# Masks as matmuls, 32-row score products and half units in the two attention stages of a hybrid layer kernel

## The chip, the cores and the metric

One core of a Trainium2 chip. The metric is the device time of one execution in microseconds, less is better. Engines are TensorE (PE in the profile, its weight loads PEld), VectorE (DVE), ScalarE (ACT), GpSimd (POOL) and the DMA queues, mostly issued by SyncE (SP). Each engine works through its own instructions strictly in program order and waits on semaphores.

## What is computed

The kernel computes a two-layer block (512 tokens, 1024 channels) and a second block with gated linear attention and experts. The change lies in the mixers of the first block, which both layers run. A projection is split into four groups: an rwkv7 recurrence (A), differential attention (B), spatial gating (C) and forgetting attention (D), each with 4 heads of 64 channels.

```python
def block(i):            # differential attention, 128 queries
    mask = key_chunk[None, :] <= q_chunk[:, None]        # chunks of 64
    s1 = jnp.einsum('bhqd,bhkd->bhqk', q1b, k1) * scale  # d = 32
    s2 = jnp.einsum('bhqd,bhkd->bhqk', q2b, k2) * scale
    p1 = jax.nn.softmax(jnp.where(mask, s1, NEG_INF), axis=-1)
    p2 = jax.nn.softmax(jnp.where(mask, s2, NEG_INF), axis=-1)
    return jnp.einsum('bhqk,bhkd->bhqd', p1 - lam * p2, v)

def block(i):            # forgetting attention
    s = jnp.einsum('bhqd,bhkd->bhqk', qb, k) * scale + (Fq[..., :, None] - F[..., None, :])
    pr = jax.nn.softmax(jnp.where(key_pos[None, :] <= q_pos[:, None], s, NEG_INF), axis=-1)
    return jnp.einsum('bhqk,bhkd->bhqd', pr, v)

def step(state, inp):    # rwkv7, one token; the kernel takes chunks of 64
    sa = jnp.einsum('bhvk,bhk->bhv', state, -kk_t)
    state = state * w_t + sa[..., None] * b_t + v_t[..., None] * k_t
    return state, jnp.einsum('bhvk,bhk->bhv', state, r_t)
```

## The kernel before

`mixers` (L1812) runs four instruction streams on every engine: attention (0), rwkv (1), the modulation rows (2) and the opening of the output projection (3). Each stream is a Python generator per engine, and `run` (L588) steps them by a list of numbers, the plan. TensorE, ScalarE and VectorE follow the same plan, so a plan entry 0 means "the next piece of attention" on all three. GpSimd has a short plan of its own.

An attention stage has 16 units: 4 heads times 4 blocks of 128 queries. Unit u looks at 1, 2, 3 or 4 blocks of 128 keys, so its tiles are 128, 256, 384 or 512 columns wide. Between two units the plan puts one or two rwkv steps (`alternate`, L1464).

**Forgetting stage.** A unit is, in time: score matmul into one of two banks (`score`, L771), on VectorE the causal mask added to the diagonal block (L995) and the row maximum (L997), on ScalarE the exponential (L899), on VectorE reciprocal (L1006) and scaling (L1009), on TensorE transposes (L807), on ScalarE the copy of them (L910), on TensorE the sum of values (L790). Plan entry u makes TensorE do scores of u+2, sums of u-1, transposes of u; VectorE mask and maximum of u+1, then scaling of u; ScalarE the exponential of u+1, then the copy of u. The rwkv steps of this stage are the `MICRO` ones (L1144 and L1150 on TensorE, two heads' worth of 64x64 matmuls, with a VectorE and a ScalarE operation behind some of them; for instance L1422 and L1430).

**Differential stage.** The same with two maps per unit, m = 0 and 1: scores L820, mask L1027, maximum L1029, exponential L925, reciprocal and mixing L1037, L1039, L1042 and L1044 ("the normalisation"), transposes L846, copy L939, sums L831. There is one bank for each map, so a score of a unit waits for the exponential of the unit before on the same map:

```python
for m, lane in enumerate(lanes(h)):
    if u >= 1:
        eng.wait_ge(df["exped"], 2 * (u - 1) + m + 1)
    eng.matmul(PS(m)[:, 0:width(u)], d_q[lane][:, i * P:(i + 1) * P], c.p[:, T_B + 2 + h // 2, 0:width(u)], ...)
```

The product is over 32 channels, but `d_q[lane]` is a 128-row tile with zeros outside its 32 rows, which GpSimd clears and fills (`spread_lanes`, L679; waits at L708 and L712). Plan entry u makes TensorE do scores of u+1, sums of u-1, transposes of u; VectorE the normalisation of u, then masks and maxima of u+1; ScalarE the copy of u, then the exponentials of u+1.

The rwkv steps of this stage are three parts for each of 8 chunks. Part A: TensorE L1245 and L1247 (and from the second chunk on an output, L1230 to L1232), then ScalarE L1329. Part B: TensorE L1255 (and an output), then VectorE L1440. Part C: TensorE L1264 and L1266, then VectorE L1444, on which the next A waits. 24 parts are spread over 17 plan entries.

Of the kernel before, what the change touches and what calls it, by code (L numbers as in the profile page):

```python
# [62 lines left out]
         ("mask_causal", 128), ("mask_chunk", 128), ("scan", 512), ("m_ld", 512), ("m_ldT", 512), ("m_loT", 512),  # L63
# [547 lines left out]
def attention_stream(c, mod, nc):  # L611
# [8 lines left out]
    fx = {n: sem(f"fx_{n}") for n in ("scored", "masked", "maxed", "exped", "inv", "scaled", "turned", "copied", "summed",  # L620
                                      "out", "zeroed", "spread")}
    df = {n: sem(f"df_{n}") for n in ("lam_dve", "lam_exp", "lam", "scored", "masked", "maxed", "exped", "inv", "mixed",
# [24 lines left out]
    d_q = [VT(V_D), VT(V_C), at["w"](7), VT(V_C + 1)]  # L647
    lanes = lambda h: [2 * h % 4, 2 * h % 4 + 1]
    d_prob, d_prob_t = [[SC(0), SC(1)], [SC(2), c.p[:, T_D, :]]], [SC(3 + i) for i in range(2)]
# [14 lines left out]
    def pool():  # L664
# [14 lines left out]
        def spread_lanes(h):  # L679
            for lane in lanes(h):  # L680
                r = slice(32 * lane, 32 * lane + 32)
                chain(eng.tensor_copy(d_q[lane][r, :], c.p[r, T_B + h // 2, :]))

# [19 lines left out]
        eng.wait_ge(pr["roped"], 3 * NJ)  # L703
        eng.wait_ge(fx["summed"], NU // 2)
        eng.memset(d_q[0], 0.0).then_inc(fx["zeroed"], 1)
        eng.wait_ge(fx["scored"], 12)
        for lane in (1, 2):
            eng.memset(d_q[lane], 0.0).then_inc(fx["zeroed"], 1)  # L708
        eng.wait_ge(fx["zeroed"], 8)
        spread_lanes(0)  # L710
        eng.wait_ge(fx["scored"], 16)
        eng.memset(d_q[3], 0.0).then_inc(fx["zeroed"], 1)  # L712
        eng.wait_ge(fx["zeroed"], 9)
        spread_lanes(1)
        yield
        for h in range(2, 4):
            eng.wait_ge(df["scored"], 8 * (h - 1))
            spread_lanes(h)
        yield

    def pe():
# [73 lines left out]
        for u in range(NU):  # L795
# [39 lines left out]
        for u in range(NU):  # L835
            if u == 0:
                score2(0)
            if u + 1 < NU:
                score2(u + 1)
# [5 lines left out]
            for b in range(blocks[u][1] + 1):  # L845
                last = eng.transpose(PS(2)[:, b * P:(b + 1) * P], d_prob[u % 2][0][:, b * P:(b + 1) * P], c.const("ident"))  # L846
            last.then_inc(df["turned"], 1)
            yield
        sum_values2(NU - 1)
# [7 lines left out]
    def act():  # L857
# [44 lines left out]
        for u in range(NU):  # L902
            if u == 0:
                exp(0)
            if u + 1 < NU:
                exp(u + 1)
            eng.wait_ge(fx["turned"], u + 1)
# [6 lines left out]
            yield  # L914
        eng.wait_ge(fx["summed"], NU)
# [3 lines left out]
        def exp2(u):  # L919
            for m in range(2):  # L920
                n = 2 * u + m
                eng.wait_ge(df["maxed"], n + 1)
                if u >= 2:
                    eng.wait_ge(df["turned"], u - 1)
                on(d_prob[u % 2][m][:, 0:width(u)], PS(m)[:, 0:width(u)], ACT.Exp, bias=d_max[:, n:n + 1],  # L925
# [7 lines left out]
        for u in range(NU):  # L933
            if u == 0:
                exp2(0)
            eng.wait_ge(df["turned"], u + 1)
# [5 lines left out]
            if u + 1 < NU:  # L942
                exp2(u + 1)
            yield
        take(1)
# [9 lines left out]
    def dve():  # L955
# [35 lines left out]
        def maximum(u):  # L991
            i = blocks[u][1]
            eng.wait_ge(fx["scored"], u + 1)
            diagonal = PS(u % 2)[:, i * P:(i + 1) * P]
            eng.tensor_tensor(diagonal, diagonal, c.const("mask_causal"), ALU.add).then_inc(fx["masked"], 1)  # L995
            eng.wait_ge(fx["masked"], u + 1)
# [3 lines left out]
        for u in range(NU):  # L1000
            if u == 0:
                maximum(0)
            if u + 1 < NU:
                maximum(u + 1)
            eng.wait_ge(fx["exped"], u + 1)
# [4 lines left out]
            yield  # L1010
        eng.wait_ge(df["lam_exp"], 1)
# [9 lines left out]
        def maximum2(u):  # L1021
            i = blocks[u][1]
# [9 lines left out]
        for u in range(NU):  # L1032
            if u == 0:
                maximum2(0)
            eng.wait_ge(df["exped"], 2 * u + 2)
# [5 lines left out]
            p1, p2 = d_prob[u % 2][0][:, 0:width(u)], d_prob[u % 2][1][:, 0:width(u)]  # L1041
# [3 lines left out]
            if u + 1 < NU:  # L1045
                maximum2(u + 1)
            yield
        yield
# [425 lines left out]

def project_in(c, lin, sums, apply, swept):
# [336 lines left out]
def mixers(c, sums, w_out, ahead):  # L1812
# [9 lines left out]
    plan = [1] * b["shift"] + [2] + [0] * a["first"]  # L1822
    plan += alternate(a["gating"] + a["prepare"], b["prepare"] + EARLY) + [2]
# [2137 lines left out]
```

## Time and profile before

| | |
|---|---|
| median of 3 runs | 2393.91 us (2390.57 to 2396.67) |
| profiled execution, its own time | 2392.87 us |
| its span | 2390.9 us |
| TensorE busy | 2185.5 us (91%) |
| VectorE busy | 1532.1 us (64%) |
| ScalarE busy | 1047.0 us (44%) |
| GpSimd busy | 121.6 us (5%) |

Busy time is the share in which an engine had an instruction running; a matmul's end is modelled and matmuls overlap, so 91% is not TensorE at its peak. The mean granted clock of TensorE was 0.964 of full speed. The change touches two stretches in each of the two layers: the forgetting stage from 240 us and the differential stage from 309.5 us, and again from 1025 and 1094.5 us.

### The profile page before, as it was taken

The page shows a single profiled execution, that of the slowest core. Times are in us where ns is not written, and L with a number is a line of the kernel's source. Part 1 is how long each engine was busy: PE and PEld are TensorE (multiplying, and loading weights), DVE is VectorE, ACT ScalarE, POOL GpSimd, SP SyncE. Part 2 cuts the span into 40 slices and gives each one's busy share as a digit, 9 for nine tenths or more (in the row PEclk, how much of TensorE's full clock was granted, in tenths as well). Part 3 has the DMA queues.
Part 4 walks back from the last instruction along what each step waited for, and adds up shares of the span by engine and source line. Part 5 has one row for each costly group of instructions (what it writes and reads, how often), then busy time and mean ns, then how long its engine had stood idle before and what let it go on. Part 6 is the DMA issues. An engine that isn't in the chain of part 4 may idle for free. (4 is left out here: it accounts for less than half of the span.)

```text
span 2390.9 us, 35471 instructions
## 1 busy us (share of the span) xinstructions
PE 2185.5 (91%) x13217; PEld 1741.9 (73%) x13217; DVE 1532.1 (64%) x2178; ACT 1047.0 (44%) x1572; POOL 121.6 (5%) x189
## 2 busy tenths in 40 slices
PE   5998888999999899888899999999997889799994
PEld 4875566788888787566678888888886666688883
DVE  6657466555577565756655557665434665799996
ACT  3444334433341335433433335133234434688884
POOL 0001200000000000110000000000001010111111
PEclk9999999999999999999999999989998999899997
DMA  8650011233335265001123333537505001899995
GB/s 320 217 185 15 2 37 45 80 96 96 96 144 187 90 211 194 24 2 37 35 74 96 96 96 126 199 96 259 186 19 176 1 19 63 340 410 417 417 414 214
DMA packets 95445, 348.53 MB, mean 146 GB/s; under 512 B 12360, under 2 KB 14520, under 8 KB 95056
## 3 DMA queue, kind: packets, MB, share of 16 engines
q1 hardware_dynamic: 88688, 323.67, 38.1%
q0 software_dynamic: 3888, 14.16, 1.5%
q10 hardware_dynamic: 2736, 8.92, 0.9%
q8 instruction: 85, 1.39, 0.2%
q14 instruction: 48, 0.39, 0.1%
HBM read 333.55 MB, written 21.54 MB: 149 GB/s over the span
## 5 line engine op out<-in xcount | busy, mean ns | idle before, releaser
L501 PE MATMUL ps<-a_hi,w_hi 128*128 128x512 f32 x1344 | 536.4, 399 | 28.4 <-DVE h_lo L407 17.6
L503 PE MATMUL ps<-a_hi,w_lo 128*128 128x512 f32 x1344 | 527.6, 393 | 0.0
L502 PE MATMUL ps<-h_lo,w_hi 128*128 128x512 f32 x1280 | 502.3, 392 | 0.0
L465 DVE TENSOR_TENSOR w_lo<-ring,w_hi 128x1024 fp32r<-128x1024 f32 x178 | 218.1, 1226 | 355.6 <-ACT w_hi L460 355.1
L460 ACT ACTIVATE w_hi<-ring 128x1024 fp32r<-128x1024 f32 x178 | 188.1, 1059 | 492.7 <-PE ps L503 487.2
L501 PEld LDWEIGHTS ps<-a_hi,w_hi 128*128 128x128 f32 x1344 | 255.5, 190 | 92.3 <-issue 26.4
L503 PEld LDWEIGHTS ps<-a_hi,w_lo 128*128 128x128 f32 x1344 | 255.3, 190 | 54.4
L502 PEld LDWEIGHTS ps<-h_lo,w_hi 128*128 128x128 f32 x1280 | 243.3, 190 | 51.8 <-issue 2.9
L3385 DVE TENSOR_TENSOR moe_w_lo<-p,moe_w_hi 128x1024 fp32r<-128x1024 f32 x204 | 238.9, 1223 | 17.3 <-ACT moe_w_hi L3482 12.1
L3482 ACT ACTIVATE moe_w_hi<-p 128x1024 fp32r<-128x1024 f32 x204 | 216.1, 1062 | 66.5 <-PE ps L3425 52.3
L2132 PE MATMUL ps<-p_lo,down_hi 128*128 128x512 f32 x352 | 137.0, 389 | 0.0
L3423 PE MATMUL ps<-moe_w_hi,moe_x_hi 128*128 128x512 f32 x272 | 108.9, 401 | 4.9 <-DVE moe_w_lo L3385 2.9
L3425 PE MATMUL ps<-moe_w_lo,moe_x_hi 128*128 128x512 f32 x272 | 107.5, 395 | 0.0
L3424 PE MATMUL ps<-moe_w_hi,moe_x_lo 128*128 128x512 f32 x272 | 107.3, 395 | 0.0
L2049 ACT ACTIVATE down_hi<-down_raw 128x1408 fp32r<-128x1408 f32 x32 | 44.1, 1379 | 142.5 <-PE ps L2133 142.5
L502 PE MATMUL ps<-y_lo,w_hi 128*128 128x512 f32 x192 | 77.2, 402 | 0.0
L2132 PEld LDWEIGHTS ps<-p_lo,down_hi 128*128 128x128 f32 x352 | 66.1, 188 | 13.6
L292 DVE SCALAR_TENSOR_TENSOR y<-vt,cond,y 128x1024 f32<-128x1024 f32 x56 | 70.7, 1280 | 5.5 <-DMA vt<-in_ada 5.5
L2053 DVE TENSOR_TENSOR down_lo<-down_raw,down_hi 128x1408 fp32r<-128x1408 f32 x32 | 52.0, 1625 | 33.8 <-ACT down_hi L2049 32.8
L1984 DVE SCALAR_TENSOR_TENSOR y<-ps,cols,y 128x510 f32<-128x510 f32 x88 | 65.9, 749 | 11.0 <-DVE y L1981 0.5
L1954 ACT ACTIVATE y<-ps,cols 128x512 f32<-128x512 f32 x88 | 67.0, 762 | 8.8 <-PE ps L503 8.8
L1960 ACT ACTIVATE y<-y 128x512 f32<-128x512 f32 x44 | 27.8, 632 | 91.3 <-DVE y L1984 91.3
(617 smaller groups left out, 3943.4 us busy)
## 6 DMA issues: line engine op xcount, KB each, us to landing
ring<-in_ffn_up SPq DMA_DIRECT2D x88, 512.0 KB, 3.6
ring<-in_w_in SPq DMA_DIRECT2D x72, 512.0 KB, 5.2
p<-in_moe_gate SPq DMA_DIRECT2D x68, 512.0 KB, 6.8
p<-in_moe_up SPq DMA_DIRECT2D x68, 512.0 KB, 7.0
p<-in_moe_down SPq DMA_DIRECT2D x68, 512.0 KB, 7.8
vt<-in_ada SPq DMA_DIRECT2D x64, 512.0 KB, 3.9
p<-in_ada SPq DMA_DIRECT2D x48, 512.0 KB, 5.7
down_raw<-in_ffn_down SPq DMA_DIRECT2D x32, 704.0 KB, 4.9
```

The lines of the kernel that those rows point to most:

```text
L292: ins = nc.vector.scalar_tensor_tensor(out, self.piece[b], factor, out, ALU.mult, ALU.add)
L460: self.c.nc.scalar.activation(self.c.w_hi[:, s % 2, :], self.c.slot(s), ACT.Copy).then_inc(self.high, 1)
L465: self.c.nc.vector.tensor_tensor(self.c.w_lo[:, s % 2, :], self.c.slot(s), self.c.w_hi[:, s % 2, :].bitcast(F32), ALU.subtract).then_inc(s ...
L501: nc.tensor.matmul(bank, c.w_hi[:, s % 2, at], hi(kt), start=(kt == self.order[0]), stop=False)
L502: nc.tensor.matmul(bank, c.w_hi[:, s % 2, at], lo(kt), start=False, stop=False)
L503: return nc.tensor.matmul(bank, c.w_lo[:, s % 2, at], hi(kt), start=False, stop=(kt == self.order[-1]))
L2132: nc.tensor.matmul(bank, down.w_hi[n % 2][:, at], c.p_lo[:, kt, :], start=False, stop=False)
L3385: ops.tensor_tensor(m.w_lo[:, n % 4, :], m.raw[n], m.w_hi[:, n % 4, :].bitcast(F32), ALU.subtract).then_inc(low[n], 1)
L3423: nc.tensor.matmul(bank, x[0], w_hi, start=start, stop=False)
L3424: nc.tensor.matmul(bank, x[1], w_hi, start=False, stop=False)
L3425: return nc.tensor.matmul(bank, x[0], w_lo, start=False, stop=stop)
L3482: nc.scalar.activation(m.w_hi[:, n % 4, :], m.raw[n], ACT.Copy).then_inc(high[n], 1)
```

## The change

It does five things.

1. The mask is no longer added by VectorE. Before each score TensorE multiplies the identity with the mask table (forgetting), or a 32-row table `first_rows` with `later_keys` (differential), into the diagonal block, and the score accumulates on it.
2. A differential score is a 32-row matmul at the lane's own rows of queries and keys, with a tile position. GpSimd's tiles `d_q`, their clearing and the copies go.
3. `maximum2`, `exp2` and `score2` run one unit further ahead, as the forgetting stage's already do, and the probabilities have three buffers instead of two.
4. Every unit is two pieces instead of one, on TensorE, ScalarE and VectorE. The first half holds scores of u+2, maximum and exponential of u+1, the second half sums, normalisation, transposes and copy.
5. `halves` builds the plan: the second half of a unit and the first half of the next stand together, and the rwkv steps stand between the two halves of a unit.

```diff
-            eng.matmul(bank, x_q[h % 2][:, i * P:(i + 1) * P], x_k[h % 2][:, 0:nk], start=True, stop=True
-                       ).then_inc(fx["scored"], 1)
+            eng.matmul(bank[:, i * P:], c.const("ident"), c.const("mask_causal"), start=True, stop=False,
+                       skip_group_check=True)
+            eng.matmul(bank, x_q[h % 2][:, i * P:(i + 1) * P], x_k[h % 2][:, 0:nk], start=False, stop=True,
+                       skip_group_check=True).then_inc(fx["scored"], 1)
...
         def score2(u):
             h, i = blocks[u]
-            if i == 0:
-                eng.wait_ge(fx["spread"], 12 + 2 * (h + 1))
             for m, lane in enumerate(lanes(h)):
                 if u >= 1:
                     eng.wait_ge(df["exped"], 2 * (u - 1) + m + 1)
-                eng.matmul(PS(m)[:, 0:width(u)], d_q[lane][:, i * P:(i + 1) * P], c.p[:, T_B + 2 + h // 2, 0:width(u)],
-                           start=True, stop=True).then_inc(df["scored"], 1)
+                r = slice(32 * lane, 32 * lane + 32)
+                eng.matmul(PS(m)[:, i * P:width(u)], c.const("first_rows")[r, :], c.const("later_keys")[r, :], start=True,
+                           stop=False, skip_group_check=True, tile_position=(32 * lane, 0))
+                eng.matmul(PS(m)[:, 0:width(u)], c.p[r, T_B + h // 2, i * P:(i + 1) * P],
+                           c.p[r, T_B + 2 + h // 2, 0:width(u)], start=False, stop=True, skip_group_check=True,
+                           tile_position=(32 * lane, 0)).then_inc(df["scored"], 1)
...
         for u in range(NU):
             if u == 0:
                 score2(0)
-            if u + 1 < NU:
-                score2(u + 1)
+                score2(1)
+            if u + 2 < NU:
+                score2(u + 2)
+            yield
             if u >= 1:
                 sum_values2(u - 1)
...
         for u in range(NU):
             if u == 0:
                 exp2(0)
+            if u + 1 < NU:
+                exp2(u + 1)
+            yield
             eng.wait_ge(df["turned"], u + 1)
...
-            if u + 1 < NU:
-                exp2(u + 1)
-            yield
...
                 eng.wait_ge(df["scored"], n + 1)
-                diagonal = PS(m)[:, i * P:(i + 1) * P]
-                eng.tensor_tensor(diagonal, diagonal, c.const("mask_chunk"), ALU.add).then_inc(df["masked"], 1)
-                eng.wait_ge(df["masked"], n + 1)
                 eng.tensor_reduce(d_max[:, n:n + 1], PS(m)[:, 0:width(u)], AXX, ALU.max, negate=True
                                   ).then_inc(df["maxed"], 1)
...
             if u == 0:
                 maximum2(0)
+            if u + 1 < NU:
+                maximum2(u + 1)
+            yield
             eng.wait_ge(df["exped"], 2 * u + 2)
...
+def halves(plan):
+
+    order, open_half = [], False
+    for i in plan:
+        if i == 0:
+            order += [0] * (1 + open_half)
+            open_half = True
+        else:
+            order.append(i)
+    return order + [0]
```

The forgetting stage gets the same extra `yield` between its halves, and its mask on VectorE goes the same way.

TensorE in the differential stage, between the transposes of two units (`ps<-k,ring` rows are the transposes, `64x64` rows rwkv part B, `64x128` rows sums of values). Before, units 1 and 2:

```order
L846 MATMUL ps<-k,ring 128x128 x2
L1255 MATMUL ps<-h,w2b 64x64 x4
L820 MATMUL ps<-p,vt 128x512 x2
L831 MATMUL ps<-ring,vt 64x128 x2
L846 MATMUL ps<-k,ring 128x128 x3
```

Now, units 0 and 1:

```order
L833 MATMUL ps<-k,ring 128x128
L802 MATMUL ps<-k 128x128
L804 MATMUL ps<-p 128x512
L802 MATMUL ps<-k 128x128
L804 MATMUL ps<-p 128x512
L1243 MATMUL ps<-h,w2b 64x64 x4
L816 MATMUL ps<-ring,vt 64x128
L833 MATMUL ps<-k,ring 128x128 x2
```

L802 is the mask matmul, L804 the score. The scores that stood behind the rwkv part, ahead of sums and transposes, now stand ahead of the rwkv part. Before, scores of unit 3 follow the transposes of unit 1; now they follow those of unit 0.

VectorE in the same stage, units 1 and 2 (L1037 to L1044 and L1026 to L1033 are the normalisation, L1029 and L1015 a maximum, L1440 and L1428 rwkv part B). Before:

```order
L1037 RECIPROCAL small<-small 128x2
L1039 TENSOR_TENSOR small<-small 128x1
L1042 TENSOR_SCALAR p<-p,small 128x256
L1044 SCALAR_TENSOR_TENSOR ring<-ring,small,p 128x256
L1027 TENSOR_TENSOR ps<-ps,k 128x128
L1029 TENSOR_REDUCE small<-ps 128x1
L1027 TENSOR_TENSOR ps<-ps,k 128x128
L1029 TENSOR_REDUCE small<-ps 128x1
L1440 COPY h<-ps 128x64 x2
```

Now:

```order
L1015 TENSOR_REDUCE small<-ps 128x1 x2
L1428 COPY h<-ps 128x64 x2
L1026 RECIPROCAL small<-small 128x2
L1028 TENSOR_TENSOR small<-small 128x1
L1031 TENSOR_SCALAR p<-p,small 128x256
L1033 SCALAR_TENSOR_TENSOR ring<-ring,small,p 128x256
L1015 TENSOR_REDUCE small<-ps 128x1 x2
L1432 SCALAR_TENSOR_TENSOR h<-h,small,ps 128x64 x2
```

The masks are gone, and the two maxima behind the normalisation of unit 1 are those of unit 3, where they were those of unit 2.

ScalarE, from the copy of unit 0 (L939 and L932 are copies, L925 and L915 exponentials, L1329 and L1317 the rwkv operation behind part A). Before:

```order
L939 ACTIVATE ring<-ps 128x128
L925 ACTIVATE ring,small<-ps,small 128x256
L925 ACTIVATE p,small<-ps,small 128x256
L1329 ACTIVATE h<-ps 128x64 x2
L939 ACTIVATE ring<-ps 128x256
```

Now:

```order
L932 ACTIVATE ring<-ps 128x128
L915 ACTIVATE p,small<-ps,small 128x384 x2
L932 ACTIVATE ring<-ps 128x256
L915 ACTIVATE ring,small<-ps,small 128x512 x2
L1317 ACTIVATE h<-ps 128x64 x2
```

Behind the copy of a unit stand the exponentials of the unit after the next, where they were those of the next.

## Rows read from the trace of the kernel before

**Rows 1.** Busy time by stretch: start:end, length, busy us of each engine, clock, DMA.

```profile
240.00:309.50 69.50, 58.16 (x985) 44.12 (x984) 31.66 (x85) 23.53 (x60) 12.26 (x19) 0.98 0.01 2
309.50:381.50 72.00, 62.31 (x700) 42.78 (x696) 50.31 (x162) 30.43 (x104) 2.66 (x6) 0.98 0.09 31
...
1094.50:1166.50 72.00, 62.31 (x700) 42.78 (x695) 50.32 (x162) 30.47 (x104) 2.66 (x6) 0.98 0.09 31
```

**Rows 2.** Timeline (start, us, engine, line): first scores, last transposes of the differential stage.

```profile
309.57 0.71 PE L820 MATMUL ps<-p,vt 128*128 128x128 f32 x4
...
376.43 0.65 PE L846 MATMUL ps<-k,ring 128*128 128x128 f32 x4 [1.17 <-DVE ring L1044]
```

**Rows 3.** Timeline, differential stage: from the exponentials of unit 2 to unit 3's.

```profile
318.20 0.57 ACT L925 ACTIVATE ring<-ps,small 128x384 f32<-128x384 f32 x1
...
318.76 0.58 ACT L925 ACTIVATE ring<-ps,small 128x384 f32<-128x384 f32 x1
...
319.46 0.17 DVE L1037 RECIPROCAL small<-small 128x2 f32<-128x2 f32 x1 [0.91 <-ACT ring L925]
319.48 0.19 PEld L820 LDWEIGHTS ps<-p,vt 128*128 128x128 f32 x1 [0.27 <-ACT ring L925]
...
320.85 0.29 DVE L1027 TENSOR_TENSOR ps<-ps,k 128x128 f32<-128x128 f32 x1
...
321.18 0.69 DVE L1029 TENSOR_REDUCE small<-ps 128x1 f32<-128x512 f32 x1
...
321.42 0.55 PE L846 MATMUL ps<-k,ring 128*128 128x128 f32 x3
...
322.39 0.68 ACT L925 ACTIVATE ring<-ps,small 128x512 f32<-128x512 f32 x1
```

**Rows 4.** Waits, differential stage: who waited for whom, us in all, times, longest.

```profile
ACT ring L939 <- PE ps L846: 39.8, 16, 3.9
POOL w2b L682 <- PE ps L820: 14.7, 1, 14.7
```

**Rows 5.** Timeline, differential stage: parts B, A and C, two scores, sums.

```profile
317.81 0.31 PEld L1255 LDWEIGHTS ps<-h,w2b 64*64 64x64 f32 x8 [0.17 <-issue]
...
318.19 0.36 DVE L1440 COPY h<-ps 128x64 f32<-128x64 f32 x2
...
368.57 0.33 PE L1245 MATMUL ps<-w2b,h 64*64 64x64 f32 x4
...
369.70 1.12 PE L820 MATMUL ps<-p,w2b 128*128 128x512 f32 x2
...
370.66 1.02 PE L820 MATMUL ps<-p,vt 128*128 128x512 f32 x2
...
373.78 0.33 PE L1264 MATMUL ps<-w2b,ring 64*64 64x64 f32 x4 [0.15 <-DVE h L1440]
...
374.28 0.52 DVE L1444 SCALAR_TENSOR_TENSOR h<-h,small,ps 128x64 f32<-128x64 f32 x2 [0.32 <-PE ps L1266]
...
378.14 1.09 PE L831 MATMUL ps<-ring,vt 128*64 128x128 f32 x8
```

**Rows 6.** Timeline, forgetting stage: an rwkv step and what follows it.

```profile
276.11 2.08 PE L1144 MATMUL ps<-ring 64*64 64x64 f32 x64
...
278.31 0.69 DVE L1422 COPY ring<-ps 128x512 f32<-128x512 f32 x1 [5.53 <-PE ps L1144]
278.92 0.29 DVE L995 TENSOR_TENSOR ps<-ps,k 128x128 f32<-128x128 f32 x1
...
280.50 0.44 PE L807 MATMUL ps<-k,ring 128*128 128x128 f32 x2 [0.89 <-DVE ring L1009]
...
282.88 0.49 PE L779 MATMUL ps<-ring,vt 128*128 128x128 f32 x2
```

**Rows 7.** Busy time by stretch, around a fall of TensorE's clock.

```profile
310.00:313.00 3.00, 1.52 (x7) 0.69 (x5) 2.30 (x9) 0.92 (x4) 0.04 (x1) 1.00 0.33 86
314.00:316.00 2.00, 2.00 (x15) 1.27 (x12) 1.24 (x5) 1.17 (x6) 0.00 (x0) 0.50 0.91 348
```

More of the change, by code:

```diff
@@ L619, in attention_stream @@
                                       "roped")}
-    fx = {n: sem(f"fx_{n}") for n in ("scored", "masked", "maxed", "exped", "inv", "scaled", "turned", "copied", "summed",
+    fx = {n: sem(f"fx_{n}") for n in ("scored", "maxed", "exped", "inv", "scaled", "turned", "copied", "summed",
                                       "out", "zeroed", "spread")}
-    df = {n: sem(f"df_{n}") for n in ("lam_dve", "lam_exp", "lam", "scored", "masked", "maxed", "exped", "inv", "mixed",
+    df = {n: sem(f"df_{n}") for n in ("lam_dve", "lam_exp", "lam", "scored", "maxed", "exped", "inv", "mixed",
                                       "turned", "copied", "summed", "squared", "ms", "rs", "out")}
@@ L646, in attention_stream @@
     own, other = [slice(0, 64), slice(64, 128)], [slice(64, 128), slice(0, 64)]
-    d_q = [VT(V_D), VT(V_C), at["w"](7), VT(V_C + 1)]
     lanes = lambda h: [2 * h % 4, 2 * h % 4 + 1]
-    d_prob, d_prob_t = [[SC(0), SC(1)], [SC(2), c.p[:, T_D, :]]], [SC(3 + i) for i in range(2)]
+    d_prob = [[SC(0), SC(1)], [SC(2), c.p[:, T_D, :]], [c.p[:, T_C + m, :] for m in range(2)]]
+    d_prob_t = [SC(3 + i) for i in range(2)]
     d_o, d_sq, d_rs = [c.p[:, T_D + 1 + t, :] for t in range(2)], [c.p[:, T_D + 3, :], SC(13)], [c.p[:, T_D, :], c.p[:, T_F, :]]
@@ L677, in spread_head @@
                 chain(eng.tensor_copy(dst[own[side], :], c.p[own[side], tile, :]))
[L679 to L682, printed above, removed]
         eng.wait_ge(sg["mixed"], 2)
@@ L702, in pool @@
             spread_head(h)
[L703 to L714, printed above, removed]
-        yield
-        for h in range(2, 4):
-            eng.wait_ge(df["scored"], 8 * (h - 1))
-            spread_lanes(h)
         yield
@@ L845, in pe @@
             for b in range(blocks[u][1] + 1):
-                last = eng.transpose(PS(2)[:, b * P:(b + 1) * P], d_prob[u % 2][0][:, b * P:(b + 1) * P], c.const("ident"))
+                last = eng.transpose(PS(2)[:, b * P:(b + 1) * P], d_prob[u % 3][0][:, b * P:(b + 1) * P], c.const("ident"))
             last.then_inc(df["turned"], 1)
             yield
+        yield
         sum_values2(NU - 1)
@@ L906, in act @@
                 exp(u + 1)
+            yield
             eng.wait_ge(fx["turned"], u + 1)
@@ L914, in act @@
             yield
+        yield
         eng.wait_ge(fx["summed"], NU)
@@ L922, in exp2 @@
                 eng.wait_ge(df["maxed"], n + 1)
-                if u >= 2:
-                    eng.wait_ge(df["turned"], u - 1)
-                on(d_prob[u % 2][m][:, 0:width(u)], PS(m)[:, 0:width(u)], ACT.Exp, bias=d_max[:, n:n + 1],
+                if u >= 3:
+                    eng.wait_ge(df["turned"], u - 2)
+                on(d_prob[u % 3][m][:, 0:width(u)], PS(m)[:, 0:width(u)], ACT.Exp, bias=d_max[:, n:n + 1],
                    accum_out=d_sum[:, n:n + 1]).then_inc(df["exped"], 1)
@@ L1004, in dve @@
                 maximum(u + 1)
+            yield
             eng.wait_ge(fx["exped"], u + 1)
@@ L1010, in dve @@
             yield
+        yield
         eng.wait_ge(df["lam_exp"], 1)
@@ L1021, in maximum2 @@
         def maximum2(u):
-            i = blocks[u][1]
             for m in range(2):
@@ L1040, in dve @@
             eng.wait_ge(df["inv"], 3 * u + 2)
-            p1, p2 = d_prob[u % 2][0][:, 0:width(u)], d_prob[u % 2][1][:, 0:width(u)]
+            p1, p2 = d_prob[u % 3][0][:, 0:width(u)], d_prob[u % 3][1][:, 0:width(u)]
             eng.tensor_scalar(p2, p2, r[:, 1:2], None, ALU.mult).then_inc(df["inv"], 1)
@@ L1821, in mixers @@
     EARLY = 8
-    plan = [1] * b["shift"] + [2] + [0] * a["first"]
-    plan += alternate(a["gating"] + a["prepare"], b["prepare"] + EARLY) + [2]
-    plan += alternate(a["forget"], b["intra"] - EARLY)
-    last = alternate(a["diff"], b["scan"])
-    at = len(last) - 1 - last[::-1].index(0)
-    plan += last[:at] + [3] + last[at:] + [3, 1, 0, 1, 3, 0, 3, 1, 3]
+    gating = [1] * b["shift"] + [2] + [0] * a["first"]
+    gating += alternate(a["gating"] + a["prepare"], b["prepare"] + EARLY) + [2]
+    forget = alternate(a["forget"], b["intra"] - EARLY)
+    diff = alternate(a["diff"], b["scan"])
+    at = len(diff) - 1 - diff[::-1].index(0)
+    end = [3, 1, 0, 1, 3, 0, 3, 1, 3]
+    plan = gating + halves(forget) + halves(diff[:at]) + [3] + halves(diff[at:]) + end
     opened = open_out_stream(c, att, rw, w_out)
@@ L1840, in _ @@
             c.sweep(pool, [*ahead.loaded, ahead.high, ahead.low])
-            run("pool", streams[:2], [0, 0, 1, 0, 1, 0])
+            run("pool", streams[:2], [0, 0, 1, 0, 1])
         @block.tensor
@@ L3941, in constants @@
     k["mask_causal"] = np.where(n[None, :] <= n[:, None], 0.0, NEG)
-    k["mask_chunk"] = np.where(n[None, :] // 64 <= n[:, None] // 64, 0.0, NEG)
+    lane = n[:, None] % 32 == 0
+    k["first_rows"] = np.where(lane & (n[None, :] < 64), 1.0, 0.0)
+    k["later_keys"] = np.where(lane & (n[None, :] >= 64), NEG, 0.0)
     k["scan"] = np.tile((np.arange(S) % CH != 0).astype(f)[None, :], (P, 1))
```

12 lines of the change are left out of this document (5 added, 7 removed).

## The prediction

> **What bounds the kernel now.** I read the division of the span into stages first. The change touches two stages of each of the two layers: the forgetting attention and the differential attention, each interleaved with the rwkv steps. [rows 1] give them as 69.5 and 72 us. The second layer repeats the first to within 0.05 us in every column, so everything below is worked out once and counted twice. TensorE shows work in 84% and 87% of these stages, VectorE in 46% and 70%, so no engine is full and only the order of waits decides.
>
> The waits say which: in the differential stage ScalarE waits 39.8 us for the transposes in 16 waits [rows 4], so it has room. The timeline of one unit [rows 3] shows the loop. The first exponential of unit 2 starts at 318.20, that of unit 3 at 322.39: a period of 4.19 us, and the 16 units stand between 309.57 and 376.43, 66.9 us or 4.18 each [rows 2]. In it the exponentials free the two score banks, the normalisation (from 319.46) follows on VectorE, and mask and maximum (from 320.85) come right behind it. Beside all that TensorE computes the next scores (from 319.48). **The scores run beside the normalisation; that is the cover to watch.**
>
> **What the change does to the differential stage.** It removes 32 masks on VectorE (0.33 us from one start to the next: mask at 320.85, maximum behind it at 321.18) and adds 32 mask matmuls. It also moves the scores. In the new order TensorE has, between two rwkv steps: sums of values of u-1, transposes of u, scores of u+3. The scores of u+3 wait for both exponentials of u+2, since there is one bank for each of the two maps. ScalarE reaches those exponentials only behind the copy of u (of the same group), VectorE the maxima of u+2 only behind the normalisation of u. And the next rwkv step stands on TensorE behind the scores, the next normalisation on VectorE behind the rwkv operation that this step feeds. So nothing runs beside anything any more: exponential, score, rwkv step, normalisation, transposes, copy, next exponential are one ring.
>
> Widths are 1 to 4 blocks of 128 columns, 2.5 in the mean; a term read at 384 columns is taken half a block lower, one read at 512 one and a half.
> - first to second exponential: 318.20 to 318.76 [rows 3], taken 0.50
> - second exponential to its score: 318.76 to 319.48, taken 0.67
> - one score: 369.70 to 370.66 at 512 columns [rows 5], less 1.5 blocks of 0.21 (1.12 us busy at 512 against 0.49 at 128, [rows 5, 6]), 0.64
> - one mask matmul, which the trace of before lacks: four 128-column matmuls of 64 weight columns take 1.09 us [rows 5], 0.27 each; a 128-column score with full weights 0.49 [rows 6]. I take 0.27, since its weights can be loaded while the engine waits for the exponential; the bounds are 0.2 and 0.49
> - change to the rwkv step: 0.17, the gap that the rwkv row of [rows 5] at 317.81 shows
> - normalisation: 319.46 to 320.85, taken 1.29
> - its end to transposes, copy and next exponential: 0.06, then 321.42 to 322.39 at 384 columns, taken 0.92 in all
>
> Without the normalisation this is 3.17 us. The rwkv part comes in three kinds [rows 5]: A occupies TensorE for 1.13 (368.57 to 369.70) and asks nothing of VectorE; B needs 0.74 until VectorE is through (317.81 to 318.19, and 0.36); C 1.02 (373.78 to 374.28, and 0.52). The 13 cycles from the exponentials of unit 2 to those of unit 15 hold:
> - B alone, 3 times: 3.17 + 0.74 + 1.29 = 5.20, 15.6
> - C alone, 3 times: 5.48, 16.4
> - A and B, twice: 3.17 + 1.13 + 0.74 + 1.29 = 6.33, 12.7
> - B and C, once: B with a handover of 0.1, then C: 6.3
> - A alone, twice: the normalisation is hidden, and TensorE's sums (2.5 matmuls of 0.27, 0.69) stand in its place: 3.17 + 1.13 + 0.69 = 4.99, 10.0
> - C and A, twice: C and a handover 1.12, then 1.13 + 0.69 + 3.17 and another gap of 0.17: 6.28, 12.6
>
> Sum 73.6 us. Ahead of it come the units 0, 1 and 2, each score behind the exponential before it and no normalisation between: two links of 0.50 + 0.67 + 0.64 + 0.27 and a maximum with its handovers (0.49 + 0.2), 2.8 each, less 0.3 because the first is narrow, and 1.4 for the first score and maximum: an estimate of 6.7 us. Behind it the units 14 and 15 have no more scores to make: two maxima of 512 columns (1.4), B and C (1.4 of it exposed), the normalisation of 14 (1.4), A (1.3) and sums (0.8), less the 0.8 by which the normalisation of 13 was ahead: about 6.0. The last transposes then start 86.3 us into the stage instead of 66.9: **+19.4 us a layer**. What follows them (copy, the first operands of the output projection) keeps its length.
>
> **The forgetting stage.** Its scores have two banks and wait for nothing. Where VectorE has an rwkv operation (12 of 16 units), the wait of TensorE for the normalised rows ends last now: rwkv product, operation at 278.31, mask at 278.92, maximum, normalisation, transposes at 280.50 [rows 6]. Mask and maximum leave that chain (0.33, and 0.49, which is the 0.69 of [rows 3] at 512 columns less 1.5 blocks of 0.13: 0.82), but the score, which was hidden in the same wait (0.64 at the mean width, and 0.1 that its first weight load shows: 0.74), comes out of it, with 0.27 for the mask matmul. Twelve times 0.82 come off, 9.8; 13 times 1.01 come on, 13.1; four units without a VectorE operation had their score on the path already, less 3.0. Near zero, and then the last sums of values (1.09 us at 4 blocks), which stood ahead of the last rwkv pair, stand alone behind it: **+1.3 us a layer**. Bounds: 0 with the mask matmul at 0.2, +4 at 0.49.
>
> **What costs nothing.** The eight copies and four clearings on GpSimd waited up to 14.7 us themselves [rows 4], which is spare time; their removal gives nothing. One more table of 128 columns rides with the start-up loads. The third probability buffer lifts a wait that the ring never reaches.
>
> **The clock.** In [rows 7] TensorE is at half clock (1.2 GHz) from 314 to 316, right after three microseconds in which it was busy for 1.52. The new stage has it waiting some 2 us in each 5.6. I add 3 us a layer, three more such dips of about 1 us on a ring of which TensorE holds half; bounds 0 and 8. The Trainium skill (TensorE: Matmul & The Clock Gate, Part 1) has the same two levels and says idleness is what lowers the clock; this row agrees.
>
> **Sum.** 19.4 + 1.3 + 3 = 23.7 a layer, 47 for two. The profiled execution took 2392.87 us (span 2390.9), within 0.05% of the median 2393.91. 2392.87 + 47 = **2440 us**.
>
> One point of this sum is open: whether the second score of a unit, which sits in another 32-row group, runs while the first still streams. The rows suggest it: 64 records of 64 columns on 64-row tiles take 2.08 us, 0.033 each [rows 6], while 8 records of 128 columns take 1.09 us, 0.136 each [rows 5], four times as long for twice the columns. I let it run, so only the second score's own time stands in the ring. If it must wait for the first, the surplus of score and mask (0.91) over the distance of the exponentials (0.50) is added 13 times: +5.3 a layer, 2451 us. The Trainium skill (TensorEngine Tiling (Array Packing), Key Properties) says that different tiles load and multiply in parallel, which would give 2440. The same skill (TensorE: Matmul & The Clock Gate, Why this matters for your kernels) says that a single matmul of 32 rows takes as long as one of 128, which speaks against a gain from the smaller scores alone; no row here has one.
>
> **The rivals.**
> 1. *The ring is not closed: faster.* If TensorE, not ScalarE, is the late one when it comes to the scores of u+3, their wait is empty, and the masks' removal counts: 0.65 us of 4.18 in each of 16 units, 10.4 a layer, 2372 us. It decides at the point where exponentials of u+2 end before the transposes of u do. For it: VectorE is 70% busy and is in today's loop. Against: those exponentials stand behind the copy that needs these very transposes.
> 2. *No change*, 2393: gain of the masks and loss of cover cancel, which needs a period of 4.2 where I count 5.6.
> 3. *Dearer: no overlap of row groups*, 2451, and with the clock at its bound, 2461.
> 4. *The halving is not what it says* (the same order as before, masks alone moved): the order of instructions excludes it.
>
> **How the numbers follow.** Forecast 0.62, rival 3 in its two sizes 0.22, a milder loss (2400 to 2420, short links where I took means) 0.06, rival 1 0.07, rival 2 0.03. A measurement of this kernel tells 0.3%, 7 us, from no change. Faster 0.07, same 0.03, slower 0.90. The range leaves out the two last rivals and the ends: 2418 to 2463.
>
> **What would show it.** In the differential stage after: its length near 91 us; the exponentials 5 to 6.5 us apart, shortest where only A stands between; TensorE's wait for ScalarE before a score going from the 0.27 of [rows 3] to about 1; VectorE's share near 45%, since 32 masks (9.3 us) are gone and the stage is longer. The forgetting stage should stay within 4 us of 69.5. The forecast is wrong if the period is near 4 us, or if the scores of a unit start without a wait for an exponential.

## The result

The changed kernel takes 2481.07 us (median of 4 runs, 2478.02 to 2485.64) against 2393.36 (4 runs): a ratio of 1.0367, 95% interval 1.0347 to 1.0388. It is 87.7 us **slower**, 43.9 a layer, where 47 and a range up to 2463 were forecast. The sign and the place are right, the size is not.

Its page, the first rows of parts 1 and 2 (the granted clock in tenths):

```profile
span 2479.3 us, 35717 instructions
PE 2248.6 (91%) x13409; PEld 1796.5 (72%) x13409; DVE 1503.2 (61%) x2082; ACT 1047.5 (42%) x1572; POOL 106.8 (4%) x165
PEclk9999956999999999997599999998999899799997
```

TensorE shows 63 us more work than before with nearly the same work to do, and the clock row has two hollows, at 5 to 7 tenths, where the two differential stages lie. Busy time by stretch, as [rows 1] gave it for before: the forgetting stage, then the differential one.

```profile
239.50:306.80 67.30, 57.96 (x1017) 45.77 (x1018) 26.72 (x68) 21.83 (x59) 7.91 (x13) 1.00 0.01 2
306.80:422.00 115.20, 92.05 (x737) 67.64 (x736) 40.76 (x132) 30.56 (x103) 0.00 (x0) 0.61 0.05 19
```

The forgetting stage is 2.2 us shorter. The differential stage, counted like the 72 us of [rows 1], has 115.2, VectorE busy in 35% of it, and a mean granted clock of **0.61**. Below a stage is counted to the end of its last transposes: 67.2 us before, 112.4 after, in both layers.

The waits of that stretch (us in all, times, longest). ScalarE waited 39.8 us for transposes in [rows 4]:

```profile
ACT ring L932 <- PE ps L833: 62.9, 15, 6.9
DVE h L1428 <- PE ps L1243: 42.1, 8, 8.1
...
PEld ps L802 <- ACT ring L915: 14.2, 10, 2.2
```

The second row's partner before was short:

```profile
DVE h L1440 <- PE ps L1255: 5.9, 3, 3.2
```

VectorE now stands at rwkv part B (L1428) with the normalisation queued behind, while TensorE is in the scores ahead of that part. The timeline from the exponentials of unit 3 to those of unit 4, the counterpart of [rows 3]:

```profile
320.14 0.68 ACT L915 ACTIVATE ring<-ps,small 128x512 f32<-128x512 f32 x1
...
320.81 0.69 ACT L915 ACTIVATE ring<-ps,small 128x512 f32<-128x512 f32 x1
...
320.97 0.79 PE L802 MATMUL ps<-k 32*128 32x128 f32 x2 [1.14 <-ACT ring L915]
...
322.79 0.48 PE L1252 MATMUL ps<-w2b,ring 64*64 64x64 f32 x4
...
323.53 0.71 DVE L1432 SCALAR_TENSOR_TENSOR h<-h,small,ps 128x64 f32<-128x64 f32 x2 [3.25 <-PE ps L1254]
...
324.15 0.16 DVE L1026 RECIPROCAL small<-small 128x2 f32<-128x2 f32 x1
...
324.99 0.62 DVE L1033 SCALAR_TENSOR_TENSOR p<-p,small 128x384 f32<-128x384 f32 x1
...
325.82 0.89 PE L816 MATMUL ps<-ring,vt 128*64 128x128 f32 x4
...
326.65 0.55 PE L833 MATMUL ps<-k,p 128*128 128x128 f32 x3
...
327.23 0.49 ACT L932 ACTIVATE ring<-ps 128x384 f32<-128x384 f32 x1 [1.98 <-PE ps L833]
327.62 0.36 ACT L915 ACTIVATE ring<-ps,small 128x128 f32<-128x128 f32 x1
```

Exponentials, scores, rwkv parts C and A, normalisation, sums, transposes, copy, exponentials: the ring of the prediction, nothing beside anything. It takes 7.48 us, nearly all at half clock. Even the sums, which at full clock end beside the normalisation, now hold the transposes up by 1 us (normalisation done at 325.61, transposes at 326.65). Busy time by stretch:

```profile
314.80:318.80 4.00, 3.45 (x16) 1.42 (x14) 1.23 (x6) 0.00 (x0) 0.00 (x0) 0.50 0.00 0
318.80:322.80 4.00, 2.52 (x12) 1.90 (x12) 1.48 (x3) 1.72 (x5) 0.00 (x0) 0.50 0.00 0
322.80:326.80 4.00, 4.00 (x50) 3.56 (x50) 2.23 (x8) 0.45 (x2) 0.00 (x0) 0.56 0.02 4
```

### The profile page after: what moved, and what is told of

It reads as the page before. It is cut to its first block and busy times, and to the rows that moved or that the text cites. A ratio compares the mean times of both kernels' runs of the same rounds, so it can differ in the third digit from the quotient of the medians.

```text
span 2479.3 us, 35717 instructions
## 1 busy us (share of the span) xinstructions
PE 2248.6 (91%) x13409; PEld 1796.5 (72%) x13409; DVE 1503.2 (61%) x2082; ACT 1047.5 (42%) x1572; POOL 106.8 (4%) x165
## 5 line engine op out<-in xcount | busy, mean ns | idle before, releaser
L1982 DVE SCALAR_TENSOR_TENSOR y<-ps,cols,y 128x511 f32<-128x511 f32 x88 | 65.5, 744 | 4.7 <-ACT y L1955 4.7
```

## The experiments

In each heading stand the edit's base, the time, the ratio to before with its interval, and the lengths of forgetting / differential stage (clock of the latter; both layers where they differ).

**1. The change to the forgetting stage alone**: 2383.78 us, 0.9955 (0.9942 to 0.9968); 67.4 / 66.3 us (1.00).

```diff
-    plan += alternate(a["forget"], b["intra"] - EARLY)
+    plan += halves(alternate(a["forget"], b["intra"] - EARLY))
```

(with the mask matmul and the yields of that stage)

> The kernel before, with the change in the forgetting stage alone (mask matmul, halves); the differential stage as before. In the profile of the whole change this stage is 67.3 us long where it was 69.6. If the stages simply add, this is 2.2 us a layer: about 2389 us, ratio 0.998. If the shorter stage hides something that comes back in the next one, 2393.

A gain, where the prediction had a loss of 1.3 a layer, and more than twice the 4.4 us expected from the stage's length: of 9.7 us in all, 6.2 lie in the four stretches.

**2. 32-row scores and masks, in the order of before** (run 1 with the change's mask matmul and 32-row score in the differential stage): 2397.11 us, 1.0013 (1.0004 to 1.0021); 67.4 / 69.1 and 69.5 (0.85).

> As e1, and in the differential stage mask matmuls and 32-row scores too, but in the order of before (scores and maxima one unit ahead, whole units). Theory 1 (the loss is the closed ring of the new order, and the clock that falls with its waits): VectorE is rid of 0.33 to 0.65 us in each of 16 units, so some 5 us a layer come off e1: about 2379 us, TensorE's clock in the differential stage near full. Theory 2 (32-row matmuls are dear in themselves: they load the array little, so the clock falls, and changing tiles costs): the differential stage is long here too, its clock near half, over 2430 us.

Neither theory: the order carries most of the loss, yet 32 masks less on VectorE gained nothing, and the clock fell from 1.00 to 0.85.

**3. The changed kernel with 128-row scores and masks**: 2453.22 us, 1.0257 (1.0233 to 1.0281); 67.4 / 97.7 (0.91).

```diff
-                r = slice(32 * lane, 32 * lane + 32)
-                eng.matmul(PS(m)[:, i * P:width(u)], c.const("first_rows")[r, :], c.const("later_keys")[r, :], start=True,
-                           stop=False, skip_group_check=True, tile_position=(32 * lane, 0))
+                eng.matmul(PS(m)[:, i * P:width(u)], c.const("first_rows"), c.const("later_keys"), start=True,
+                           stop=False, skip_group_check=True)
...
+                eng.matmul(PS(m)[:, 0:width(u)], d_q[lane][:, i * P:(i + 1) * P], c.p[:, T_B + 2 + h // 2, 0:width(u)],
+                           start=False, stop=True, skip_group_check=True).then_inc(df["scored"], 1)
```

> The changed kernel with 128-row scores and 128-row mask matmuls in the differential stage (zero-padded tiles made by GpSimd as before), order and halves as changed. Theory 1: the ring is the same and the two scores of a unit no longer overlap, so at least as slow as the change, 2480 to 2510 us, clock of the stage again near 0.6. Theory 2: the clock comes back and the stage shrinks by 15 us or more a layer, 2450 us or less.

Scores that can't overlap, from the same banks in the same order, and the kernel is 28 us faster than the change: theory 2 in the main, 3 us short of it. The stage by stretch, then a ring of its timeline, at full clock:

```profile
312.00:409.70 97.70, 71.49 (x693) 51.64 (x692) 39.74 (x127) 28.06 (x98) 2.43 (x4) 0.91 0.06 23
```


```profile
318.82 0.57 ACT L937 ACTIVATE p<-ps,small 128x384 f32<-128x384 f32 x1
...
319.54 0.49 PE L825 MATMUL ps<-k 128*128 128x128 f32 x2 [0.93 <-ACT p L937]
...
321.90 0.45 PE L1265 MATMUL ps<-h,w2b 64*64 64x64 f32 x8
...
322.55 0.15 DVE L1048 RECIPROCAL small<-small 128x2 f32<-128x2 f32 x1
...
324.57 0.38 ACT L954 ACTIVATE ring<-ps 128x256 f32<-128x256 f32 x1 [4.53 <-PE ps L855]
324.85 0.68 ACT L937 ACTIVATE ring<-ps,small 128x512 f32<-128x512 f32 x1
```

Scores to part B 0.65 us, normalisation to the next exponential 2.30: forecast 0.74, and 1.29 + 0.92. The head, 318.82 to 321.90, is 3.08 with exponentials of 384 and scores of 512 columns, the widest of all; the sum's 2.25 is for the mean width and for overlapping scores.

**4. The changed kernel, differential units whole** (look-ahead and 32-row matmuls kept): 2464.96 us, 1.029 (1.027 to 1.0311); 67.4 / 106.6 and 105.0 (0.57, 0.59).

> The changed kernel, but in the differential stage the two halves of a unit stand together and the rwkv parts between units, scores, maxima and exponentials still further ahead. Then the scores run beside the normalisation again, but the exponentials they wait for are still in the same group. Theory 1: by the same terms a period of about 5.1 us at full clock, 82 us for the stage instead of 112: about 2420 us, more if the clock still falls. Theory 2: still a 32-row stage at half clock, 2460 us or more.

Theory 2, in time and in clock. The halves are not the main cause.

**5. Run 2 with 128-row scores and masks**: 2393.61 us, 1.0004 (0.9994 to 1.0014); 67.5 / 70.3 (1.00).

> As e2 (forgetting stage changed; differential stage in the order of before, masks by TensorE) but with 128-row scores and 128-row mask matmuls. Theory A (the 32-row matmuls let the clock fall, and that is what e2 lost against e1): clock of the differential stage at full, VectorE rid of 32 masks, stage 62 to 66 us against 66.3 in e1: 2375 to 2384 us. Theory B (masks on TensorE are what costs, whatever their rows): no faster than e2, 2395 us or more.

Theory B. With the clock at 1.00, masks on TensorE instead of VectorE still cost 4.0 us a layer against run 1.

**6. The changed kernel with four 128-row matmuls into the bank of the transposes, ahead of each wait for the normalised rows and behind the wait for the copy of the unit before**: 2483.17 us, 1.0376 (1.0361 to 1.0391); 67.4 / 116.1 and 108.4 (0.74, 0.81).

> The changed kernel with four more 128x128 matmuls of the identity per differential unit, into the bank of the transposes, while TensorE waits for the normalised rows; they add 0.9 us of work a unit at full clock, and leave the output as it is. Theory A, in the form that the clock follows how much of the array works: more wide work raises the clock of the stage from 0.61 to 0.75 or more and the time falls, below 2475 us. Theory C (the waits alone lower the clock): the waits get shorter too, so the clock rises as well, but then e3, whose waits are as long, should not have kept 0.91. If neither, the filler only costs: 2490 us or more.

The clock rose as theory A has it, and the time did not fall. The filler stands in the ring: in the timeline the normalised rows of a unit are ready at 322.59 (322.11 and 0.48), and the transposes start 1 us later, behind filler (L831) that takes 2.08 us at half clock. Where the filler runs at full clock it can be over in time, so how much of the gain it eats in all is not shown.

```profile
321.69 2.08 PE L831 MATMUL ps<-k 128*128 128x128 f32 x8
...
322.11 0.48 DVE L1034 SCALAR_TENSOR_TENSOR ring<-ring,small,p 128x256 f32<-128x256 f32 x1
...
323.56 0.63 PE L834 MATMUL ps<-k,ring 128*128 128x128 f32 x2
```

**7. Run 3 with the exponentials ahead of the copy on ScalarE**: 2433.14 us, 1.0162 (1.0148 to 1.0177); 67.4 / 88.3 and 86.6 (0.90, 0.92).

> e3 (changed order, 128-row scores, clock mostly full) with the exponentials of a unit ahead of the copy that stood before them on ScalarE. The ring then goes normalisation, maximum, exponential instead of normalisation, transposes, copy, exponential. If the ring is as I hold it: about 0.4 us off each of 13 periods, 5 us a layer, 2443 us. If the stage is bound by TensorE or by the rwkv chain: unchanged, 2453 us.

One link out of the ring, twice the forecast gain.

**8. Run 7 with the maxima first on VectorE and the scores first on TensorE**: 2433.36 us, 1.0167 (1.0151 to 1.0183); 67.4 / 86.8 and 88.4 (0.94, 0.90).

> e3 with maxima, exponentials and scores each ahead of normalisation, copy and sums in their group, so that the scores run beside the normalisation again; still halves, one unit further ahead. If the ring is what costs: the stage falls from 98 us to 70 to 78, in all about 2400 to 2415 us. If the further look-ahead or the position of the rwkv parts costs: it stays above 2435 us.

A miss: nothing gained. TensorE now stands at the scores, which wait for the exponentials of the same group, before it comes to the rwkv part, so the part runs behind the exponentials again. That this eats just what the earlier maxima gain is argued, not shown.

**9. Run 3 with the scores one unit less ahead, halves kept**: 2408.89 us, 1.0076 (1.0057 to 1.0094); 67.4 / 74.8 (1.00).

```diff
-            if u + 2 < NU:
-                score2(u + 2)
+            elif u + 1 < NU:
+                score2(u + 1)
```

> e3 (changed order, 128-row scores) with the differential scores one unit less ahead, so that a score waits for exponentials of the group before, which run beside the rwkv part; halves kept. Ahead theory (it is the wait for exponentials of the same group that serialises the stage): the stage falls from 97.7 us to 72 to 78, in all 2400 to 2412 us. Halves theory (the rwkv part between maximum and normalisation is what costs): stage over 90 us, 2440 us or more.

Ahead theory, in stage and time: 23 us a layer come back.

**10. Run 3 with whole units, look-ahead kept**: 2428.44 us, 1.0154 (1.0137 to 1.0171); 67.4 / 83.9 and 87.9 (0.96, 0.90).

> e3 with whole units in the differential stage (rwkv parts between units), the look-ahead kept. Ahead theory: the exponentials and the rwkv part are still one behind the other, so most of the loss stays: stage 85 to 98 us, 2430 to 2453 us. Halves theory: the stage is back near the 70.3 us of e5, about 2400 us.

Nearer the ahead theory, though a little shorter than it said; the 70.3 us of the halves theory are far off.

Runs 5, 9, 10 and 3 are a square at 128 rows: 70.3 us with neither, 74.8 with halves, 83.9 to 87.9 with the look-ahead, 97.7 with both. The look-ahead costs 14 to 18 us alone and 23 on halves. A part of that is the clock, which is 1.00 in runs 5 and 9 and 0.90 to 0.96 in the two with the look-ahead.

**11. 32-row scores alone, in the order of before, masks on VectorE** (run 1, `d_q` replaced): 2397.90 us, 1.0033 (1.0013 to 1.0054), with its own runs between 2389.75 and 2412.97; profiled 67.4 / 71.7 and 82.2 (0.79, 0.63).

> e1 with 32-row scores in the differential stage and nothing else: masks on VectorE, order of before, no GpSimd tiles. If 32-row matmuls let the clock fall in any order: clock of the stage below 0.95 and the stage longer than the 66.3 us of e1, 2386 to 2395 us. If they do so only in a stage that waits much: clock near 1.00, and the overlap of the two scores takes up to 0.4 us off a unit, 2375 to 2384 us.

Clock and stage are as the first theory has them, the time is 3 us above it. The profiled execution took 2412.12 us, 14 more than the median, so its stages are longer than those of a middle one. The order is that of run 1, which had 66.3 us at 1.00. Busy time by stretch of the second layer's differential stage, run 1, then run 11:

```profile
1086.90:1153.20 66.30, 56.35 (x602) 37.81 (x600) 48.77 (x159) 26.99 (x96) 2.43 (x4) 1.00 0.09 33
```

```profile
1098.20:1180.40 82.20, 75.62 (x602) 51.45 (x600) 49.68 (x159) 26.69 (x96) 0.00 (x0) 0.63 0.07 27
```

TensorE shows work in 92% of the stage against 85%, and has the lower clock (which itself makes its matmuls last longer). At full clock, timeline of run 11, the four records of two 512-column scores:

```profile
1151.40 1.13 PE L802 MATMUL ps<-p 32*128 32x512 f32 x4
1152.46 0.65 PE L814 MATMUL ps<-ring,vt 128*64 128x128 f32 x4
```

1.13 us for both, where [rows 5] has 369.70 to 371.68, 1.98: the two scores do run beside each other.

**12. Halves in the forgetting stage, nothing else** (run 1 with the causal mask back on VectorE): **2379.36 us**, 0.9946 (0.9932 to 0.9960); 64.6 / 66.2 (1.00).

> e1 with the causal mask back on VectorE; halves kept. With halves mask and maximum stand in the shade of the rwkv step, so the mask costs VectorE nothing there, and TensorE is rid of a mask matmul of 0.2 to 0.3 us in each of 16 units: stage 63 to 66 us instead of 67.4, 2375 to 2382 us. If the mask on VectorE delays the next rwkv operation, 2384 us or more.

Within both ranges expected, and the fastest version measured. VectorE behind an rwkv product, timeline (before: 278.31 and 278.92 of [rows 6]):

```profile
275.50 0.69 DVE L1428 COPY ring<-ps 128x512 f32<-128x512 f32 x1 [4.44 <-PE ps L1150]
276.11 0.15 DVE L1011 RECIPROCAL small<-small 128x1 f32<-128x1 f32 x1
276.30 0.29 DVE L1014 TENSOR_SCALAR ring<-ring,small 128x128 f32<-128x128 f32 x1
276.50 0.29 DVE L999 TENSOR_TENSOR ps<-ps,k 128x128 f32<-128x128 f32 x1
276.83 0.56 DVE L1001 TENSOR_REDUCE small<-ps 128x1 f32<-128x384 f32 x1
```

The normalisation comes straight behind the rwkv operation, mask and maximum after it.

**13. The changed kernel with 128-row scores, masks left at 32 rows**: 2513.11 us, 1.0494 (1.0456 to 1.0532); 67.4 / 122.9 and 133.5 (0.72, 0.64).

> The changed kernel with 128-row scores, its mask matmuls left at 32 rows. Theory A, the 32-row score takes the clock down, the small mask matmul does not: clock of the differential stage near 0.9, its length 97 to 101 us, time 2450 to 2460. Theory B, any 32-row matmul does: clock 0.6 to 0.75, length 105 to 112 us, time 2467 to 2481.

The small mask matmul alone takes the clock down, as theory B has it, but the stage is longer than either theory said. Its pairs run one after the other, as in run 3, and each takes longer. The first mask of two pairs of 512 columns and the rwkv part behind them, at full clock:

```profile
314.58 0.48 PE L826 MATMUL ps<-k 32*128 32x128 f32 x2 [0.93 <-ACT p L938]
...
317.52 0.45 PE L1266 MATMUL ps<-h,w2b 64*64 64x64 f32 x8
```

2.94 us, where run 3 has 2.36 (319.54 to 321.90): going from 32 rows to 128 and back costs about 0.3 us a pair. For 16 units that is 9 us a layer at full clock and more at half, by an estimate. It takes theory B's 112 to 121 or more, near the first layer's 122.9; the second layer's 133.5 stays in part open.

**14. The changed kernel with 128-row masks, scores left at 32 rows**: 2541.59 us, 1.062 (1.0604 to 1.0636); 67.4 / 139.8 and 140.8 (0.56, 0.55).

> The changed kernel with 128-row mask matmuls, its scores left at 32 rows. Theory A, the score is the cause: clock stays at 0.6 to 0.7, time 2475 to 2485. Theory C, 128-row work anywhere between the waits holds the clock up: clock 0.85 or more, time near 2455.

The clock is theory A's, the time is nobody's: the slowest of all. Two pairs of 512 columns in its timeline, then two in that of the changed kernel, both at half clock:

```profile
321.05 0.80 PE L802 MATMUL ps<-k 128*128 128x128 f32 x2 [0.93 <-ACT p L915]
...
321.78 2.07 PE L804 MATMUL ps<-p 32*128 32x512 f32 x2
...
323.78 0.80 PE L802 MATMUL ps<-k 128*128 128x128 f32 x2
...
324.50 2.07 PE L804 MATMUL ps<-p 32*128 32x512 f32 x2
...
326.51 0.69 PE L1243 MATMUL ps<-h,w2b 64*64 64x64 f32 x8
```

```profile
313.95 1.14 PE L802 MATMUL ps<-k 32*128 32x128 f32 x3 [0.93 <-ACT p L915]
...
315.10 1.91 PE L804 MATMUL ps<-p 32*128 32x512 f32 x3
316.94 0.69 PE L1243 MATMUL ps<-h,w2b 64*64 64x64 f32 x8
```

5.46 us against 2.99. One 128-row matmul between the two scores undoes their overlap, and the stage is 27 to 28 us longer; the going back and forth of run 13 and the somewhat lower clock are part of that. But 2.99 is more than the 2.36 (319.54 to 321.90) of two 128-row pairs at full clock in run 3: that is how the change gives its overlap back.

**15. The TensorE mask in the forgetting stage, units whole**: 2385.46 us, 0.9966 (0.9952 to 0.9979); forgetting 67.1, differential 66.5 (1.00).

> The kernel before with the causal mask of the forgetting stage made by TensorE and units whole. With halves, the TensorE mask cost 2.8 us a layer (67.4 against 64.6 us). If the two parts of the change add up, the forgetting stage is 69.6 + 2.8 = 72.4 us and the time near 2398. The rival: in the order of before mask and maximum stand in front of the normalisation on VectorE and the score is hidden in TensorE's wait, so here the mask matmul is covered and the mask on VectorE is what the chain loses, 12 times 0.33 = 4 us a layer: stage near 65.6, time near 2385.

The time is the rival's 2385, the stage not quite: its gain is 2.5 us where 4 were expected. The two parts don't add: from 69.6 us the mask gives 2.5, halves 5.0, both together 2.2.

## Why the prediction was wrong in size

**Right: the ring.** The same three stretches as in the forecast, of the changed kernel, from 306.80 over the first exponentials of units 2 and 15 to the last transposes:

```profile
313.23 0.57 ACT L915 ACTIVATE p<-ps,small 128x384 f32<-128x384 f32 x1
...
411.51 0.68 ACT L915 ACTIVATE ring<-ps,small 128x512 f32<-128x512 f32 x1
```

```profile
418.83 0.66 PE L833 MATMUL ps<-k,ring 128*128 128x128 f32 x4
```

| us | forecast, full clock | run 3, 128 rows, 0.91 | changed, 32 rows, 0.61 |
|---|---|---|---|
| to the exponentials of unit 2 | 6.7 | 6.8 | 6.4 |
| 13 periods | 73.6 | 84.9 | **98.3** |
| to the last transposes | 6.0 | 5.6 | 7.3 |
| sum | 86.3 | 97.3 | 112.0 |

(run 3: from 312.00 over 318.82 and 403.74 to 409.31.) Ahead and behind what was put down holds within 1.3 us. (The terms listed for the stretch behind add up to 5.5, not 6.0, and those of the forgetting stage to 1.4, not 1.3; neither matters for the range.) For scores that don't overlap the prediction had a surcharge of 5.3, so 78.9 for the 13 periods of run 3 at full clock. Its clock of 0.91 means half clock in 18% of the stage, and TensorE holds some 3 us of a period there (two pairs at the mean width 1.8, by 1.94 at 384 columns; rwkv 0.8; transposes 0.45): 13 x 3 x 0.18 is 7, an estimate, and 78.9 + 7 = 86 against 84.9. In sum the links are right.

**Right: the overlap.** The open point went as forecast. The change at full clock, early in its stage, two pairs of 384 columns, timeline:

```profile
310.47 0.48 PE L802 MATMUL ps<-k 32*128 32x128 f32 x2 [0.76 <-ACT ring L915]
...
311.99 0.33 PE L1233 MATMUL ps<-w2b,h 64*64 64x64 f32 x4
```

1.52 us from the first mask to the rwkv part, against 1.94 in run 3. From the second exponential (0.60 earlier than its mask at 310.92) the rest is 1.07, forecast 1.08. The Trainium skill (TensorEngine Tiling (Array Packing), Key Properties) says that tiles work in parallel; runs 11 and 14 agree, with 1.13 against 1.98 and 2.99 against 5.46 us.

**Wrong: the clock.** The failed step is "I add 3 us a layer, bounds 0 and 8". With the overlap the full-clock forecast of 73.6 should stand; 98.3 were measured, so that the term is about 25 us a layer, and it alone carries the time out of the range. The size fits, by an estimate: of each period some 2.3 us are TensorE's (scores 1.08, rwkv 0.8, transposes 0.45), a mean of 0.61 means half clock in 78% of the stage, and 13 x 2.3 x 0.78 is 23; sums that come out of hiding add to it. With 25 for 3, 1.3 more at the end, 0.3 less ahead and the forgetting stage's error of 3.5, the forecast of 23.7 a layer becomes 43.2, against 43.9 measured. The cause was right for the smaller part only. I put the clock down to waits. Run 3 waits in the same places and has no 32-row matmul: its 13 periods are 6 us above the forecast at full clock (84.9 against 78.9), inside the bounds of 0 and 8. The other 19 us come with something else: run 11 has the waits and the order of before and falls to 0.79 and 0.63; run 13 has the GpSimd copies and falls, so that their absence is not it. What goes with a low clock in all of these is a **32-row matmul** in the stage: runs 2, 4, 6, 11, 13, 14 and the change itself, 0.55 to 0.85, against 0.90 to 1.00 in the runs without. It is not every matmul on a part of the array: the forgetting stage, full of 64-row rwkv matmuls, has 0.98 to 1.00 in all runs. Whether it is the number of rows, or something that goes with their tile position, was not tried. The Trainium skill (TensorE: Matmul & The Clock Gate, Part 1) ties the clock to how busy the engine has been; in run 11 the stage with TensorE busy in 92% had the lower clock than the one with 85%, so the busy share that the profile shows doesn't foretell it. Why 32 rows lower the clock stays open.

**Wrong, in sign: the forgetting stage.** Forecast +1.3, measured -2.2. The chain was read rightly (run 12's timeline), and the mask matmul came at 2.8 us between runs 12 and 1 where 13 x 0.27 = 3.5 were put down. Halves alone gave 5.0 where these terms give 2.2. A part of that is a dip of the clock at the stage's end, which the kernel before has and the others don't:

```profile
300.00:309.50 9.50, 9.50 (x208) 8.65 (x206) 3.08 (x9) 2.61 (x5) 0.00 (x0) 0.84 0.01 2
```

A third of 9.5 us at half clock is worth about 1.5 us. The rest is open.

**What would show it.** The ring came as said; the stage, near 91 us in the forecast, is 115.2. The periods, forecast at 5 to 6.5 us, were 5.3 to 6.8 in ten of the thirteen of run 3 (7.3 to 8.5 in the others), and 6.0 to 9.1 in the change. The wait before a unit's first score is 0.93 and 1.14 us, about the 1 forecast, but the 0.27 that it was set against is the wait of a second score. The first one waited 0.66 before:

```profile
318.92 1.98 PE L820 MATMUL ps<-p,vt 128*128 128x512 f32 x4 [0.66 <-ACT ring L925]
```

VectorE's share is 35% and not 45 because the stage is longer. That the removal of the GpSimd copies gives nothing is not shown: every run without them has 32-row matmuls. Masks off VectorE gained nothing in the differential stage: run 5 shows that moving them to TensorE costs 4.0 us a layer, where my rival 1 counted 10.4 as gained.

Per layer the loss of 43.9 then divides so: masks on TensorE +4.0 (run 5 less run 1), look-ahead and halves +27.4 (run 3 less run 5, some 6 of it the clock of run 3), 32-row matmuls +14.7 (112.4 less 97.7, the gain of the overlap already in it), forgetting stage -2.2, and -0.9 by which the differential stage of run 1 is shorter than before's. That is 43.0; the rest lies outside the two stages, where dips of the clock fall elsewhere. The same shows in run 1: 3.1 us a layer in the stages, 9.7 in all.

## What to carry to other kernels

Running an operation further ahead pays only if the buffer it writes is free by then; with one bank a map, a score placed before the rwkv part drags that part, and the normalisation behind it, into a ring with its own exponentials. Before packing a matmul into 32 rows, look at the granted clock of a stretch that has such matmuls: the overlap is real, but here the clock took back more than it gave. If some matmuls of a group are packed, pack those between them too. And split a change that bundles five edits: one of them (halves in the forgetting stage) was worth 0.5% by itself, and hid in a loss of 3.7%.

## What the runs showed of the hardware

- Two 32-row scores in different row groups run beside each other: 1.13 us for two of 512 columns, 1.98 at 128 rows. A 128-row matmul between them makes them serial (5.46 against 2.99 us at half clock).
- Going between 32-row and 128-row matmuls costs time even where nothing could overlap: two pairs of a 128-column mask and a 512-column score took 2.94 us at full clock with 32-row masks (run 13), 2.36 with 128-row ones (run 3).
- A stage with 32-row matmuls had a mean granted clock of 0.55 to 0.85, the same order with 128-row operands 0.90 to 1.00 (run 3 against the change, 10 against 4, 5 against 2, 1 against 11).
- Four extra 128-row matmuls a unit raised the clock from 0.61 to 0.74 and 0.81, and the time did not fall (run 6).
- The clock of such a stage varies: 71.7 us at 0.79 in one layer of run 11, 82.2 us at 0.63 in the other.
